# State space layer: TensorE's products of the skip and tap blocks with u, put one projection tick behind the products that make the taps

## What is computed

```python
def s5_mixer(x, w_in, lam_re, lam_im, log_dt, b_re, b_im, c_re, c_im, d_skip, w_glu, b_glu, w_out):
    u, z = jnp.split(x @ w_in, 2, axis=-1)            # projection, 256 x 2048 @ 2048 x 2048
    ...                                               # ar, ai, bbar from lam, dt, b
    bu_r = jnp.einsum('lbgc,gpc->lbgp', ug, bbar_r)
    bu_i = jnp.einsum('lbgc,gpc->lbgp', ug, bbar_i)
    _, _, h_r, h_i = lax.associative_scan(_complex_linear_combine, (ar.., ai.., bu_r, bu_i), axis=0)
    y = einsum('gcp,lbgp->lbgc', c_re, h_r) - einsum('gcp,lbgp->lbgc', c_im, h_i)
    y = y + d_skip * u
    g = jax.nn.gelu(y)
    y = g * jax.nn.sigmoid(g @ w_glu + b_glu)
    return (y * jax.nn.silu(z)) @ w_out
```

## Time and profile before

| | |
|---|---|
| median of 3 runs | 2066.75 us (2063.72 to 2066.98) |
| the profiled execution's own time | 2066.16 us |
| its span, first to last instruction | 2064.4 us |
| PE matmul busy | 2031.5 us, 98% of the span |
| DVE busy | 1302.9 us, 63% |
| ACT busy | 975.1 us, 47% |
| mean granted TensorE clock | 0.997 |

### The profile page before, as it was taken

The page is one execution under the profiler, slowest core; times in us unless marked ns, Lnnn a source line. Parts: engine busy times, 40 slices in busy tenths (PEclk is TensorE's granted clock), DMA queues, the critical chain, the costliest instruction groups (busy, mean ns, idle before and its releaser), DMA issues.

```text
span 2064.4 us, 31959 instructions
## 1 busy us (share of the span) xinstructions
PE 2031.5 (98%) x12513; PEld 1790.0 (87%) x12513; DVE 1302.9 (63%) x1770; ACT 975.1 (47%) x1414; POOL 82.1 (4%) x84
## 2 busy tenths in 40 slices
PE   8999999999999999999999999999999999999998
PEld 7898898888989898889899898888888888888886
DVE  6799775456666666658666666556546555655555
ACT  5554554344444445446446546544434434434443
POOL 2000042000000000100000001000000000000000
PEclk9999999999999999999999999999999999999999
DMA  9245567545455554755554554566666666566663
GB/s 284 93 132 180 178 206 223 171 139 169 141 164 151 155 162 137 243 173 165 164 166 150 163 154 152 195 185 191 193 190 190 192 194 184 187 199 184 192 192 106
DMA packets 202936, 360.87 MB, mean 175 GB/s; under 512 B 25361, under 2 KB 33905, under 8 KB 202161
## 3 DMA queue, kind: packets, MB, share of 16 engines
q1 hardware_dynamic: 200656, 351.88, 55.2%
q0 software_dynamic: 1664, 5.97, 0.9%
q10 hardware_dynamic: 480, 1.10, 0.1%
HBM read 356.03 MB, written 2.10 MB: 173 GB/s over the span
## 4 chain that ended last, share of the span: by engine, by line
PE 91%; DVE 5%; ACT 2%; issue 2%; DMA 0%; ACTq 0%; POOL 0%; POOLq 0%; DVEq 0%
PE acc L517 36%; PE acc L521 19%; PE banks L517 8%; PE banks L1113 6%; PE acc L1113 6%; PE banks L1116 3%; PE acc L1116 3%; DVE w_high_low L1766 1%; PE acc L607 1%; PE banks L910 1%; PE banks L882 1%; PE acc L548 1%; ACT w_high_low L1157 1%; PE banks L999 1%; PE banks L977 1%
## 5 line engine op out<-in xcount | busy, mean ns | idle before, releaser
L1766 DVE TENSOR_TENSOR w_high_low<-raw,w_high_low 128x1024 fp32r<-128x1024 f32 x648 | 794.6, 1234 | 605.0 <-ACT w_high_low L1157 603.8
L1157 ACT ACTIVATE w_high_low<-raw 128x1024 fp32r<-128x1024 f32 x648 | 682.0, 1059 | 731.9 <-PE acc L517 325.9
L521 PE MATMUL acc<-x_high_low,w_high_low 128*128 128x256 f32 x3648 | 454.4, 285 | 0.7 <-issue 0.7
L521 PEld LDWEIGHTS acc<-x_high_low,w_high_low 128*128 128x128 f32 x3648 | 443.6, 192 | 3.5 <-issue 2.2
L517 PE MATMUL acc<-w_high_low,x_high_low 128*128 128x512 f32 x1728 | 413.9, 396 | 1.1 <-DVE w_high_low L1766 1.1
L517 PEld LDWEIGHTS acc<-w_high_low,x_high_low 128*128 128x128 f32 x1728 | 322.2, 188 | 68.1 <-issue 1.8
L517 PE MATMUL acc<-w_high_low,h_high 128*128 128x512 f32 x1088 | 292.6, 391 | 2.9 <-DVE w_high_low L1766 1.0
L517 PEld LDWEIGHTS acc<-w_high_low,h_high 128*128 128x128 f32 x1088 | 202.7, 188 | 45.9 <-issue 2.0
L517 PE MATMUL acc<-w_high_low,h_low 128*128 128x512 f32 x544 | 167.7, 389 | 0.0
L1113 PE MATMUL acc<-x_high_low,w_high_low 128*128 128x512 f32 x512 | 161.2, 396 | 1.5 <-DVE x_rows L2119 1.1
L1113 PE MATMUL banks<-x_high_low,w_high_low 128*128 128x512 f32 x512 | 160.8, 395 | 0.0
(11 more groups left out here) (362 smaller groups left out, 1639.1 us busy)
## 6 DMA issues: line engine op xcount, KB each, us to landing
raw<-in_b_w_in SPq DMA_DIRECT2D x128, 512.0 KB, 3.8
raw<-in_w_mlp_in SPq DMA_DIRECT2D x128, 512.0 KB, 3.7
raw<-in_w_mlp_out SPq DMA_DIRECT2D x128, 512.0 KB, 4.6
raw<-in_w_in SPq DMA_DIRECT2D x96, 512.0 KB, 3.8
raw<-in_kv_w SPq DMA_DIRECT2D x48, 512.0 KB, 4.0
raw<-in_a_w_in SPq DMA_DIRECT2D x32, 512.0 KB, 5.9
raw<-in_b_w_out SPq DMA_DIRECT2D x32, 512.0 KB, 4.6
raw<-in_w_out SPq DMA_DIRECT2D x32, 512.0 KB, 4.6
```

What stands on the lines that cost most here:

```text
L521: ins_ = nc.tensor.matmul(ACC[pair][:, m // 2, (m % 2) * TOK:(m % 2 + 1) * TOK], wa[:, k, j, m * P:(m + 1) * P], xa[:, kt + j, :], start=f ...
L1157: nc.scalar.activation(WH[:, s % SPLIT, :, :], RAW[:, s, :, :], ACT.Copy).then_inc(hi_ready, SLOTS + 1 if first_one else 1)
L1766: V.tensor_tensor(WL[:, k, :, :], RAW[:, p % SLOTS, :, :], WH[:, k, :, :].bitcast(F32), ALU.subtract).then_inc(lo_ready, SLOTS + 1 if isin ...
```

## The change

`taps(q)` is cut in two. The products that make the taps (L688) stay behind ticks 11, 18, 24 and 30. What followed them, the waits for `diag_ready`, `gelu_done` and the tap copy, and the products with u (2 of the skip diagonals, 6 of the tap blocks) with their signal `taps_done`, becomes `inside(q)`, which hangs behind ticks 12, 19, 25 and 31. Nothing else is edited: ACT, DVE, GpSimd and SyncE have the same instructions in the same order.

```diff
             ins_.then_inc(ring_full, 1)
+
+        def inside(q):
+
             pe.wait_ge(diag_ready, q + 1)
             if q:
                 pe.wait_ge(gelu_done, q)
@@
                 bu(0)
             if tau == 11:
                 taps(0)
+            if tau in (12, 19, 25, 31):
+                inside((12, 19, 25, 31).index(tau))
             if tau == 15:
                 b_turn(1)
```

## The result

| | before | changed |
|---|---|---|
| median of 20 runs | 2066.22 us (2063.7 to 2067.52) | 2068.28 us (2067.38 to 2069.66) |
| ratio | | 1.0014, 95% interval 1.0008 to 1.002 |
| the profiled execution, its span | 2066.16, 2064.4 | 2067.38, 2065.6 |

The forecast was 2068.6 us. The interval lies clear of 1, so the change is slower by a small amount (the ratio is estimated from all the runs; the two medians alone give 1.0010).

A forecast was written before the change was run, and what follows sets the result against it. DVE was taken to bound the opening of the GLU ticks, and PE the time from there. Opening -0.1 and clock +2.0 gave +1.9 us on the median 2066.75, so 2068.6 us; range 2064.5 to 2071.5.

The forecast's parts named there:

- The place that decides: At the opening of the GLU ticks: DVE sets it, PE's own 8 us saved before 165 count nothing, opening moves -0.1 us.
- First quarter, +2.1 us on DVE: First quarter: ACT's diagonals wait behind tick 12, so the whole DVE chain comes 2.1 us late.
- Second quarter at full clock, b_turn(2) at 108.65: Second quarter: tap products run at full clock after tick 19, so b_turn(2) starts at 108.65 instead of 112.10.
- DVE's low part at 128.4: On DVE ahead of 128.50: shrinking waits of 1.09 and 1.17 us give back the 2.1 us delay, with 0.1 over.
- PE's lead of 3.4 us: On PE at b_turn(2): 2.3 us ahead after tick 19, plus 1.2 from two further ticks at full clock.
- The gap of 5.8 us and the fall of the clock: Ahead of the first GLU tick: PE idles 5.8 us, the clock falls from 162.3 to 169.1, costing 2.0 us.
- Rival A: At the GLU ticks: the clock doesn't fall, only the -0.1 us is left, 2066.6 us; chance 0.15.
- Rival B: On DVE: the 2.1 us delay isn't given back, opening at 167.3, 4.1 us more with the clock, 2070.9 us; chance 0.12.

The follow-up runs named there:

- e2: The changed kernel with the first quarter undone (products with u behind ticks 11, 19, 25, 31): 2066.35 us, ratio 1.0004 to the kernel before.
- e3: The kernel before with only the first quarter's products with u moved (behind ticks 12, 18, 24, 30): 2068.25 us, ratio 1.0014.
- e4: The changed kernel with the first quarter undone and 14 unused filling matmuls ahead of the first GLU tick: 2064.07 us, ratio 0.9997 to the kernel before.
- e5: The kernel before with 11 unused matmuls filling the second quarter's wait for the tap copy: 2063.83 us, ratio 0.9996.
- e10: The kernel before, unchanged, profiled once more: 2063.43 us.
- e6: The kernel before with only the second quarter's products with u moved (behind ticks 11, 19, 24, 30): 2064.14 us, ratio 1.0.
- e7: The kernel before with only the last quarter's products with u moved (behind ticks 11, 18, 24, 31): 2067.88 us, ratio 1.0008; its profiled execution 2063.63 us.
- e12: The kernel before with only the last quarter's products with u moved, a single profiled execution of the same kernel as e7: 2065.14 us.
- e9: The kernel before with only the last quarter's products with u moved, a single profiled execution of the same kernel as e7: 2069.97 us.
- e1: The changed kernel with 20 unused matmuls of 512 columns filling the gap ahead of the GLU ticks: 2066.45 us, ratio 1.0003 to the kernel before.
- e11: The kernel of e1 (changed kernel, gap ahead of the GLU ticks filled), a single profiled execution: 2064.52 us.

## Why the prediction was right

- **The place that decides** (DVE opens the GLU ticks, PE's own gain is not counted): right. PE's waits fell as worked out, and the opening moved by 0.06 us (aligned) where -0.1 was forecast.
- **First quarter, +2.1 us on DVE**: 2.2 measured. e2 shows it apart, with an opening 2.2 us earlier; e3 shows 1.2 of it at the opening and 1.75 between medians, with half given back and a shorter fall of the clock.
- **Second quarter at full clock, b_turn(2) at 108.65**: aligned 108.81. DVE's low part at 128.4: aligned 128.55. The gain and the delay cancel, as said, and e2 and e4 show that the two are of one size, 2.2 us.
- **Where that gain came from.** The prediction took it from PE's lead of 3.4 us, most of it from doing tick 19 inside the wait (2.3 us) and the rest from ticks at full clock (1.2). e5 and e10 show that keeping the clock up is by itself worth all of it at the opening: with the wait left in place and no fall, the GLU ticks open at 163.09 aligned, and e2, which has the moves of the other three quarters, opens at 163.10. So against an execution without the fall these moves bring nothing there.
- **The gap of 5.8 us and the fall of the clock**: gap 5.49 (PE's last product ended at 159.8 aligned, 0.5 us later than worked out, and the opening came 0.2 later than 165.1). The fall ran from 162.4 to 169.2 aligned, where 162.3 to 169.1 was said. It cost 1.70 us, the lower end of the 1.7 to 2.3 that were given. I took 2.0, the middle, to allow for a fall up to 1.4 us later, and that did not happen. The loss per us at the low clock was 0.43 in the prediction, and is 1.70 / 3.9 = 0.44 here. By the halving that the Trainium skill gives (TensorE: Matmul & The Clock Gate, Part 1), 3.9 us of work would cost 1.95, an estimate; the measured 1.70 decides.
- **What was luck.** The two profiled executions differ by 1.76 us once aligned (0.06 + 1.70), and 1.9 was forecast for that. The medians differ by 2.06. That this is as near is partly chance: each median is taken over groups of runs, the changed kernel's lies 0.9 us over its profile, which no trace explains, and the median of the kernel before was 2066.22, 2066.5 and 2065.16 us in its three sets of runs.
- **What was missed.** I took the profiled execution for the kernel before. It is one of two kinds, the one in which the clock falls at 98, and the other costs 2.7 us less in its profile (e10). The median stood near the dear kind because that is more frequent. The changed kernel showed no such cheap kind: its 5.49 us gap brought the clock down in the profiled execution, and none of its 20 runs is below 2067.38. Against the cheap kind the change costs some 4.5 us at its median (2068.28 against about 2063.8), against the dear kind about 1.4. In the traces the opening is 2.2 us later than in e10 (aligned 165.32 against 163.09), which is the whole of the first quarter's delay, and the clock adds 1.70: 3.9 us. Rival A (no fall at the GLU ticks) was put at 0.15, with the argument that a pure idle time of 2.48 us "sufficed" before; e10 shows that it suffices only sometimes. In the two profiles with a gap of 5.5 us (changed kernel, e2) the clock fell both times.
- **Rival B** as priced (4.1 us more) did not come, as the lead at b_turn(2) was there. e3 is part of its mechanism without the lead. Against the cheap kind of the kernel before, which has most of that lead already (`b_turn(2)` at 109.45 aligned in e10, not 112.10), the first quarter's delay does stay, and the 3.9 us above are close to the price.

## What to carry to other kernels

Here, moving work out from behind a wait did not remove idle time on an engine that another one paces; it moved the idle time to the next hand-over. Ask how long that gap becomes and whether TensorE is the bound right behind it: 5.5 us of idle time ahead of dense work cost 1.7 us of clock, while a fall in a stretch with spare time (e6) cost nothing at the next hand-over. Ask also who waits for the work that was moved: ACT's diagonals did, and DVE behind them, for 2.2 us. And where a wait of 2 to 2.5 us stands ahead of dense TensorE work, look at several executions before taking one trace as "the" kernel before.

## What the runs showed that I had not expected

- A gap of about 2 to 2.5 us brings the clock down in some executions of one and the same program and not in others: 2.48 us did (before) and 2.47 did not (e10), 2.34 did not (e7) and did (e12). 5.47 and 5.49 us did in both profiled executions. The fall can come when PE already works again: at 167.7 with work from 166.23 on (e9).
- One fall of the clock saves time. In e1 the clock fell at 319.5, in a product on DVE's low parts, and behind that PE needed no waits for them: from the group at 316.92 to the next projection at 324.88 are 7.96 us. In the changed kernel, at full clock and with waits of 1.02, 1.03 and 1.11 us, the same stretch takes 327.31 - 318.25 = 9.06.

```profile
316.92 1.21 PE L813 MATMUL banks<-w_high_low,kv_cmp 128*120 128x256 f32 x8 [0.69 <-DVE w_high_low L1774]
319.15 5.71 PE L813 MATMUL banks<-w_high_low,kv_cmp 128*120 128x256 f32 x32 [1.02 <-DVE w_high_low L1774]
```

```profile
318.25 1.21 PE L810 MATMUL banks<-w_high_low,kv_cmp 128*120 128x256 f32 x8 [0.69 <-DVE w_high_low L1771]
320.48 3.48 PE L810 MATMUL banks<-w_high_low,kv_cmp 128*120 128x256 f32 x24 [1.02 <-DVE w_high_low L1771]
324.99 1.21 PE L810 MATMUL banks<-w_high_low,kv_cmp 128*120 128x256 f32 x8 [1.03 <-DVE w_high_low L1771]
327.31 5.05 PE L517 MATMUL acc<-w_high_low,x_high_low 128*128 128x512 f32 x21 [1.11 <-DVE w_high_low L1771]
```

  The first fence is e1, the second the changed kernel. All three profiled executions with a fall near 319 (e1, e5, e11) take 7.96 or 7.97 us for this stretch, and all eleven without it 9.05 or 9.06. e1's runs fit: its four cheapest (2064.87 to 2065.32 us) have a mean clock of 0.998, and its five with 0.999 lie at 2066.43 to 2066.94 (the other two have 0.998 as well, at 2066.67 and 2068.01).

  GpSimd's timeline shows where the time comes from, e1 first, then the changed kernel:

```profile
321.08 1.43 POOL L2770 TENSOR_TENSOR x_rows<-x_rows,gain_bias_half 128x512 f32<-128x512 f32 x1 [3.06 <-PE banks L813]
323.86 2.03 POOL L2768 TENSOR_TENSOR x_rows<-x_rows,gain_bias_half 128x512 f32<-128x512 f32 x1 [1.34 <-PE banks L813]
```

```profile
321.82 2.03 POOL L2767 TENSOR_TENSOR x_rows<-x_rows,gain_bias_half 128x512 f32<-128x512 f32 x1 [2.48 <-PE banks L810]
324.04 2.04 POOL L2765 TENSOR_TENSOR x_rows<-x_rows,gain_bias_half 128x512 f32<-128x512 f32 x1 [0.18 <-PE banks L810]
```

  In the trace of the kernel before, the 620 of DVE's 648 low parts that have no GpSimd work beside them take 1.21 to 1.23 us, and those of 2.3 us all have some. In the changed kernel GpSimd's two operations follow each other closely, and two low parts in a row take 2.32 and 2.30 us (from 322.62 and 324.86). In e1 the slower PE releases the second operation later (6.94 us into the stretch, not 5.79), the two low parts take 2.31 and 1.21 us, and the 1.1 us saved are that difference. That is read from the traces; no run tried it apart.
